# Reordering the opening of a two-layer diffusion backbone: order of loads, sums of squares, root, casts and low parts

## The reference

```
mod = split(silu(c) @ ada_w[0] + ada_b[0], 6)          # mod[0] shift, mod[1] scale
y   = x * rsqrt(mean(x * x, -1) + 1e-6) * norm1_g[0]
h   = y * (1 + mod[1]) + mod[0]
z   = gelu(h @ w_in)                                   # 1024 x 4096: halves u and v
v   = rmsnorm(z_v) ...;  y = (z_u * mixed(v)) @ w_out
```

## Time and profile before

| | |
|---|---|
| median of 3 runs | 1839.9 us (1839.88 to 1840.04) |
| the profiled execution's own time | 1837.93 us |
| its span, first to last instruction | 1836.1 us |
| mean granted TensorE clock | 0.999 |
| busy share PE, DVE, ACT, POOL | 99%, 83%, 53%, 25% |
| DMA, mean over the span | 205 GB/s |

### The profile page before, as it was taken

How to read it: one execution, slowest core, us unless ns; L and a number is a source line. 1 busy time by engine, 2 the same in 40 slices (tenths; PEclk the granted TensorE clock), 3 DMA queues, 4 the chain that set the end, 5 groups by cost and what they waited for, 6 DMA issues and landing times.

```text
span 1836.1 us, 35178 instructions
## 1 busy us (share of the span) xinstructions
PE 1822.6 (99%) x11716; PEld 1584.0 (86%) x11716; DVE 1520.1 (83%) x2819; ACT 966.7 (53%) x1631; POOL 454.0 (25%) x229
## 2 busy tenths in 40 slices
PE   8999999999999999999999999999999999999998
PEld 7999988888888888888889998888888888888887
DVE  6775889989998888888888589998999888885555
ACT  6754455665555444445555545565555544445554
POOL 6046588950000000000000368893000000000000
PEclk9999999999999999999999999999999999999999
DMA  9866455556554555588874455556655555555553
GB/s 383 330 237 220 161 187 191 184 199 218 203 179 163 182 172 176 186 308 320 323 254 161 161 170 184 191 185 207 218 194 171 171 173 174 180 172 194 193 190 132
DMA packets 104327, 376.40 MB, mean 205 GB/s; under 512 B 12481, under 2 KB 12737, under 8 KB 104001
## 3 DMA queue, kind: packets, MB, share of 16 engines
q1 hardware_dynamic: 103248, 373.11, 59.1%
q0 software_dynamic: 432, 2.10, 0.3%
q10 hardware_dynamic: 576, 0.32, 0.1%
HBM read 374.43 MB, written 1.05 MB: 204 GB/s over the span
## 4 chain that ended last, share of the span: by engine, by line
PE 91%; DVE 4%; DMA 2%; ACT 1%; POOL 1%; issue 0%; SPq 0%; ACTq 0%; DVEq 0%; POOLq 0%
PE ring L1882 22%; PE O L1935 13%; PE O L1937 13%; PE O L1936 13%; PE ring L1880 6%; PE ring L1887 6%; PE ring L1844 3%; PE ring L1587 2%; PE ring L1588 2%; PE ring L1589 2%; DMA raw<-in_u 2%; PE ring L1870 2%; PE ring L1849 1%; PE O L1870 1%; DVE wL L959 1%; ACT wH L574 1%
## 5 line engine op out<-in xcount | busy, mean ns | idle before, releaser
L574 ACT ACTIVATE wH<-raw 128x1024 fp32r<-128x1024 f32 x597 | 633.3, 1061 | 789.6 <-DMA raw<-in_v 361.6
L959 DVE TENSOR_TENSOR wL<-raw,wH 128x1024 fp32r<-128x1024 f32 x384 | 470.1, 1224 | 171.0 <-ACT wH L574 166.2
L1882 PE MATMUL ring<-hX,wH 128*128 128x512 f32 x1984 | 482.6, 393 | 0.0
L1882 PEld LDWEIGHTS ring<-hX,wH 128*128 128x128 f32 x1984 | 362.0, 188 | 69.5 <-issue 0.7
L1935 PE MATMUL O<-wH,gateH 128*128 128x512 f32 x1024 | 402.3, 393 | 0.2
L1937 PE MATMUL O<-wH,gateL 128*128 128x512 f32 x1024 | 398.9, 390 | 0.0
L1936 PE MATMUL O<-wL,gateH 128*128 128x512 f32 x1024 | 398.5, 389 | 0.0
L526 POOL TENSOR_TENSOR wL<-raw,wH 128x1024 fp32r<-128x1024 f32 x128 | 321.3, 2519 | 46.7 <-ACT wH L574 45.7
L1937 PEld LDWEIGHTS O<-wH,gateL 128*128 128x128 f32 x1024 | 192.2, 188 | 40.7
L1936 PEld LDWEIGHTS O<-wL,gateH 128*128 128x128 f32 x1024 | 192.4, 188 | 39.2
L1935 PEld LDWEIGHTS O<-wH,gateH 128*128 128x128 f32 x1024 | 192.3, 188 | 39.2 <-DVE gateL L1459 0.6
(11 more groups left out here) (227 smaller groups left out, 2469.4 us busy)
## 6 DMA issues: line engine op xcount, KB each, us to landing
raw<-in_u SPq DMA_DIRECT2D x256, 512.0 KB, 3.2
raw<-in_v SPq DMA_DIRECT2D x256, 512.0 KB, 3.3
ada_v<-in_ada SPq DMA_DIRECT2D x40, 512.0 KB, 4.4
raw<-in_w_q SPq DMA_DIRECT2D x30, 512.0 KB, 3.2
ada_m<-in_ada SPq DMA_DIRECT2D x24, 512.0 KB, 5.2
raw<-in_w_in SPq DMA_DIRECT2D x23, 512.0 KB, 4.3
ada_f<-in_ada SPq DMA_DIRECT2D x16, 512.0 KB, 15.1
raw<-in_w_out SPq DMA_DIRECT2D x16, 512.0 KB, 3.6
```

Source lines behind the costliest of these rows:

```text
L574: nc.scalar.activation(wH[s % RAW][:, :], (place or raw[s % RAW])[:, :], ACT.Copy).then_inc(s_h, 1)
L959: nc.vector.tensor_tensor(wL[s % RAW][:, :], raw[s % RAW][:, :], wH[s % RAW][:, :].bitcast(fp32), ALU.subtract).then_inc(s_low, 1)
L1882: ins = mm(bank[:, :], wH[s][:, k * P:k * P + P], hX[:, k, :, :].rearrange("p two t -> p (two t)"), start=(not low_weights_first and k == ...
```

## The change

The tokens come in two transfers of four tiles each, with a semaphore each, and ScalarE waits for each half before its squares. VectorE adds squares in four instructions, (0,1), (2,3), (4,5) and then the first two sums, and PE averages four tiles (3, 5, 6, 7) in place of eight; the six fillers before the means are gone. ScalarE takes the root before the cast of g0. For k = 0 VectorE multiplies token, gain and inverse root in one instruction, and ScalarE's scaling is left out. VectorE takes the ada sums earlier against the low parts of h. GpSimd makes half tiles in the order (0,s,0), (1,s,0), (0,s,1), (1,s,1), (2,s,0), (2,s,1), and PE counts them in that order. ScalarE's casts of g12 to g15 wait for PE too. SP issues f0 before g0, g4, g7 and g10 two places earlier, g12 before m16 and m17, g13 before m18, g14 before m19, and the six small loads after g15.

```
-            sp.dma_start(XT[:, :, :], xt_d).then_inc(s_x, 16)
+            for x in range(2):
+                sp.dma_start(XT[:, 4 * x:4 * x + 4, :], xt_d[:, 4 * x:4 * x + 4, :]).then_inc(s_x[x], 16)
             for g in range(4):
+                load_front(4 * g)
                 if g == 0:
                     load_gate(0)
-                load_front(4 * g)
                 load_front(4 * g + 1)
-                load_gate(3 * g + (g == 0))
+                if g:
+                    load_gate(3 * g)
+                load_gate(3 * g + 1)
                 load_front(4 * g + 2)
                 load_front(4 * g + 3)
-                if g:
-                    load_gate(3 * g + 1)
                 load_gate(3 * g + 2)
-            for dst, src in small_loads:
-                sp.dma_start(dst, src).then_inc(s_small, 16)
             m = ADA_FRONT
             for t in range(BLOCK_TILES, 16):
+                load_gate(t)
                 if t == BLOCK_TILES:
                     load_early(m)
                     m += 1
                 if t < BLOCK_TILES + 3:
                     load_early(m)
                     m += 1
-                load_gate(t)
+            for dst, src in small_loads:
+                sp.dma_start(dst, src).then_inc(s_small, 16)
...
-                    for t in range(BLOCK_TILES):
-                        front_low(t)
+                    for s in range(4):
+                        for half in range(2):
+                            front_low(3 * s, half)
+                            front_low(3 * s + 1, half)
+                        for half in range(2):
+                            front_low(3 * s + 2, half)
...
-            act.wait_ge(s_x, 16)
             for j in range(KT):
+                if j % 4 == 0:
+                    act.wait_ge(s_x[j // 4], 16)
                 square(j)
+            root(0)
             split_high(W_V, 0, 0)
-            root(0)
...
-                act.wait_ge(s_rooted, k + 1)
-                act.wait_ge(s_gain, 2 * k + 1)
-                nc.scalar.activation(sq[:, k, :], sq[:, k, :], ACT.Copy, scale=gs[:, 0, k:k + 1]).then_inc(s_xn, 1)
+                if k:
+                    act.wait_ge(s_rooted, k)
+                    act.wait_ge(s_gain, 2 * k + 1)
+                    nc.scalar.activation(sq[:, k, :], sq[:, k, :], ACT.Copy, scale=gs[:, 0, k:k + 1]).then_inc(s_xn, 1)
...
+            for n, (a, b) in enumerate(((0, 1), (2, 3), (4, 5), (1, 3))):
+                dve.wait_ge(s_sq, b + 1)
+                if n == 3:
+                    dve.wait_ge(s_pairs_sq, 2)
+                nc.vector.tensor_tensor(sq[:, b, :], sq[:, a, :], sq[:, b, :], ALU.add).then_inc(s_pairs_sq, 1)
             dve.wait_ge(s_row, 2)
...
             ada_front(0)
+            inverse_root(0)
             ada_front(1)
-            inverse_root(0)
-            dve.wait_ge(s_x, 16)
+            for x in range(2):
+                dve.wait_ge(s_x[x], 16)
             dve.wait_ge(s_rstd, 1)
-            rooted(0)
+            dve.wait_ge(s_gain, 1)
+            nc.vector.scalar_tensor_tensor(sq[:, 0, :], XT[:, 0, :], gs[:, 0, 0:1], O[1][:, 0:T], ALU.mult,
+                                           ALU.mult).then_inc(s_xn, 1)
             rooted(1)
+            low_h(0, 0)
             ada_front(2)
-            low_h(0, 0)
             ada_front(3)
-            for k in (2, 3, 4):
+            for k in (2, 3):
                 rooted(k)
             low_h(0, 1)
+            for k in (4, 5, 6, 7):
+                rooted(k)
             ada_front(4)
-            for k in (5, 6, 7):
-                rooted(k)
             ada_front(5)
-            for k in range(3, KT):
-                low_h(0, k - 1)
+            ada_front(6)
+            low_h(0, 2)
+            ada_front(7)
+            low_h(0, 3)
+            for k in range(4, KT):
                 ada_front(2 * k)
                 ada_front(2 * k + 1)
-            low_h(0, KT - 1)
+                low_h(0, k)
...
-                    pe.wait_ge(s_first_l, 2 * n + kk + 1)
+                    pe.wait_ge(s_first_l, 6 * s + (4 + kk if g == 2 else 2 * kk + g) + 1)
...
-            keep_clock(6)
-            for j in range(KT):
-                mean(0, j)
+            for j in (3, 5, 6, 7):
+                pe.wait_ge(s_sq, j + 1)
+                if j < 6:
+                    pe.wait_ge(s_pairs_sq, {5: 3, 3: 4}[j])
...
```

More of the change, by code:

```diff
@@ L196, in build @@
         s_bias = sem("s_bias")
-        s_x = sem("s_x")
+        s_x = [sem(f"s_x{x}") for x in range(2)]
         s_keys = sem("s_keys")
@@ L236, in build @@
         s_rooted = sem("s_rooted")
+        s_pairs_sq = sem("s_pairs_sq")
         s_xn = sem("s_xn")
@@ L513, in low_out, with front_low @@
                 nc.gpsimd.tensor_tensor(wL[s][:, :], raw[s][:, :], wH[s][:, :].bitcast(fp32), ALU.subtract).then_inc(s_l1, n)
-            def front_low(t):
+            def front_low(t, half):
                 pool.wait_ge(s_h, t + 1)
[L518 to L521, removed]
+                at = half * HALF
+                src = front_raw[t - 3] if t in FRONT_RAW else raw[t % RAW]
+                nc.gpsimd.tensor_tensor(wL[t % RAW][:, at:at + HALF], src[:, at:at + HALF],
+                                        wH[t % RAW][:, at:at + HALF].bitcast(fp32), ALU.subtract).then_inc(s_first_l, 1)
             def low_whole(base, i, s):
@@ L638, in front_high @@
             def front_high(t):
+                if t >= RAW:
+                    act.wait_ge(s_pe, t - RAW + 1)
                 if t in FRONT_RAW:
                     act.wait_ge(s_fraw[t - 3], 16)
-                    if t >= RAW:
-                        act.wait_ge(s_pe, t - RAW + 1)
                     nc.scalar.activation(wH[t % RAW][:, :], front_raw[t - 3][:, :], ACT.Copy).then_inc(s_h, 1)
@@ L1734, in _ @@
                     ins.then_inc(s_row, 1)
-            keep_clock(6)
-            for j in range(KT):
-                mean(0, j)
+            for j in (3, 5, 6, 7):
+                pe.wait_ge(s_sq, j + 1)
+                if j < 6:
+                    pe.wait_ge(s_pairs_sq, {5: 3, 3: 4}[j])
+                for tt in range(TT):
+                    ins = mm(O[tt][:, 0:P], sq[:, j, tt * P:tt * P + P], mean_w[:, :], start=(j == 3), stop=(j == KT - 1))
+                    if j == KT - 1:
+                        ins.then_inc(s_ms, 1)
             keep_clock(6)
@@ L1751, in _ @@
                         if s == 0:
-                            pe.wait_ge(s_rooted, KT)
+                            pe.wait_ge(s_rooted, KT - 1)
                         gate_block(2, s, 0)
```

## The result

| | before | after |
|---|---|---|
| median of 6 runs each, same chip | 1840.57 us (1839.88 to 1841.56) | 1848.21 us (1846.11 to 1853.59) |
| the profiled execution | 1837.93, span 1836.1 | 1850.07, span 1848.3 |
| mean granted clock | 0.999 | 0.997 |

The ratio is 1.0041, with a 95% interval of 1.0031 to 1.0052: slower by 7.6 us, where the forecast was 1844.0 with a range up to 1846.4. The sign and the place (the wait for u0) were right; the loss is almost twice as large.

What follows compares the result with a forecast made beforehand. Bound: u0, late behind a full queue. Late u0 and slips +2.4, clock fall +1.7, together +4.1 on the profiled 1837.93: 1842.0; the median lies 2.0 above that execution, so 1844.0 us, range 1840.6 to 1846.4.

Steps and rivals of the forecast that it cites:

- The sign and the place: Slower, chance 0.50; PE waits for u0 and starts the up projection at 65.7, 2.1 us later than before.
- The bound: Before the up projection: u0 comes late behind a full queue, so a sooner front gains 0.44 us at most.
- The means at the lower level: PE's opening: 16 passes at 0.234 us, 3.7 in all, means done at 11.8.
- ScalarE's start on the activation of k = 2: On the way to block (0,1,1): ScalarE starts at 23.6, activation at 24.4, cast of tile 4 at 25.4.
- Block (0,1,1): Middle of the front: starts at 28.1 instead of 28.98, between 26.2 and 29.0, waiting for a low half of tile 3.
- the second fall: Before the up projection: PE idles 2.9 us and the clock falls, costing 1.7, between 0 and 3.0.
- the rival of two falls: The clock falls also at the stop before block (0,1,1), delaying g12 and u0 by 1.5: +5.6, 1845.5 us, chance 0.08.
- Opening: Start of the kernel: the first half of the tokens lands 1.28 us earlier, at 5.0; the squares end at 7.6.
- The first block: PE's first gate block, after the means: at 15.8 instead of 16.78, with ends of 13.6 and 17.
- The first fall: A clock fall at PE's stop before block (0,1,1), delaying g12 and u0 by 1.5; a rival, chance 0.08.
- the restart: Queue dry from 43.4, g12 issued at 43.6 and landing 3.2 later; engines start again at 45.5, 2.1 us lost.
- the term of 0.4: Queue behind g15: the large small loads, six issues later, add some 0.4 us to u0's landing at 63.3.

Runs made afterwards that it cites:

- e2: Changed kernel with the tokens in one transfer again, all else as changed; median 1849.17 us, ratio 1.0045 to the kernel before.
- e6: Kernel before with only the tokens split into two transfers; ratio 1.0003 to the kernel before.
- e7: Changed kernel with the tokens in one transfer and SP's late loads in the order of before; ratio 1.0016 to the kernel before.
- e4: Changed kernel with 14 filler matmuls on PE ahead of the up projection, where it waits for u0; median 1846.68 us, ratio 1.0032.
- e9: e7 with 14 matmuls of one column added in the pause before the means; 1844.2 us, ratio 1.0016 to the kernel before.
- e11: e7 with the means as before: six fillers, eight tiles averaged, no additions on VectorE; ratio 1.0001 to the kernel before.
- e1: Changed kernel with SP's late loads back in the order of before; median 1845.27 us, ratio 1.0021 to the kernel before.
- e3: Kernel before with only SP's late loads in the new order; median 1846.42 us, ratio 1.0040 to the kernel before.
- e13: Kernel before with 20 front fillers replaced by 6 wider ones of the same total columns, TensorE's program 14 instructions shorter; ratio 1.0010.

## Why the prediction was too small, by its own steps

**What held.** The bound (u0 behind a full queue), the mechanism (g12's wait holds loads that need none; the queue runs dry; u0 late; PE stops; the clock falls), the low half for which block (0,1,1) waits, and ScalarE's start on the activation of k = 2 (23.6 forecast, 23.60). The means at the lower level (3.7 forecast, 3.76) held too, in part by luck: the same opening ran them at the full level in e2.

**Which steps failed.** Three in front of the up projection, and one that was missing. The changed kernel's profile gives the sizes of the three. Block (0,1,1) came 1.2 later than forecast, and a fall of the clock that had a chance of 0.08 cost 1.6 there; 0.3 was made up, so that g12 was issued at 46.12 in place of 43.6. From there u0 took 1.2 longer than the sum had. Together the up projection starts at 69.48 in place of 65.7, 5.9 later than before; with 1.5 for the second fall that is the 7.4 of 74 us, where the forecast was 4.1. What came is the rival of two falls, priced at 5.6, with 1.2 more for the block and 1.2 more for the queue, less 0.6 that was made up or came out smaller.

**Opening: a landing that was assumed.** The first half of the tokens was put 1.28 earlier, at 5.0. It landed at 6.15, when the whole had landed before (6.29); by itself this cost no time (e6). The first block, 16.25 for 15.8, lies inside the ends given; that the same opening can end between 14.9 and 17.5 is what e2 and e7 add.

**Block (0,1,1): a term mis-sized.** From 23.6 I took 0.8 to the end of the activation of k = 2. Gain, scaling, shift and activation stand in a row on ScalarE: 1.98 by the rows above, 23.60 to 25.58. Everything behind slipped: 29.26 for 28.1, and the 0.9 that g12 was to gain was gone.

**The first fall: given 0.08.** A stop of 1.9 before that block was followed by a fall in five of the seven profiles that have it (the changed kernel, e2, e4, e9, e11; not e1 and e7), a stop of 1.3 to 1.5 in none of six. Of stops inside the kernel the rows of before had shown only that 1.43 is survived, and those at its end that a fall can follow 1.23. "Only 0.7 longer than a stop that was survived" was therefore no argument for a chance under one half. What sets the two apart from the five stays open.

**The queue: the restart and the term of 0.4.** From the issue of g12 to the cast of u0 the prediction had 19.7 us (63.3 less 43.6). The four profiles with the late order took 20.4 to 22.5: the changed kernel 20.9, e3 the most. The landings of e3 show where it goes. From g11 to g12 there are 3.75 between landings, 2.5 more than a tile's 1.28, where the sum for the dry queue was 2.1. Behind that I let the transfers run at their old pace, with 0.4 for the little loads. From g12 to u0 e3 took 18.75 us for 12 tiles, 15.4 at 1.28 each (the changed kernel 17.1). Of the 3.4 lost, 1.8 stand at `bs` and `ws`, directly behind the four little loads (before, behind a full queue, the three tiles around the same loads lost 0.3); 0.6 at a tile during which an instruction packet of 16 KB ran. The rest is spread over tiles that SP issued one by one, each after its wait.

**The second fall: right.** It was in the forecast at 1.7; by the matmuls it cost 1.5. e4 takes it away, and its profile is 2.1 nearer to before at 75 us (5.3 behind in place of 7.4), 0.6 of which is an earlier u0.

**What was in no step.** The change takes 14 instructions out of TensorE's program ahead of loops that come 400 us later. I counted what the means cost in time and not that the program moves. By e13 that is 1.2 us [0.2, 3.5].

**The sum again.** By the medians: late loads 5.9 (e3), the program's length 1.2 (e13), the token split 0.3 or nothing (e6): 7.4 of 7.6. That this comes out so well is luck. By the ratios the same three are 7.4, 1.8 and 0.6, more than the whole, and each has an interval 3 to 5 us wide. Nor do the parts add up elsewhere: taking the late order out of the changed kernel (e1) gains 2.9 and not 5.9, and e7, with the additions, the level of the means, the half-tile order and the shorter program, is 3.5 above before and not the 1.2 of e13. So what these other parts cost is not settled.

## What to carry to other kernels

A load that must wait belongs behind every load that need not, on a queue that runs in order; and once such a queue has run dry, count not only the latency of the restart (2.5 here) but a slower pace after it (1.8 and 3.4 over 12 tiles here). Before a chain through several engines is priced, write down each instruction of it on the engine that is late: four short ones were priced as little more than one here. Where a gain ends in a wait for a transfer that is late already, as at u0, look first at what the edit does to that transfer.

## What the hardware showed that was not expected

- The program's own code moves over the same DMA engines as the data. A 16 KB packet of the instruction queue mostly took 0.9 to 1.3 us, and in the front of before the tile landing beside one (18.25) came 2.62 behind the tile ahead of it in place of 1.28. Behind 80 us every issue of a load that took SP more than 0.7 us, 41 in sixteen profiles, overlapped such a packet. Where the packets fall moved with 14 instructions in the front, and a wait 400 us later with them (e9, e13).
- Each fall of the clock in the middle of these runs lasted 3.41 us. It cost 1.5 to 1.6 where PE worked all through it, in e3 1.3, where PE stood still for its first 0.6.
- A matmul of one column cost 0.213 us a pass at the lower level (5.97 for 28 passes in e9), as much as the fillers of 128 columns there (2.52 for 12 in e1).
- The first half of a transfer cut in two landed at 6.15 to 6.33 (four profiles), the whole at 6.19 to 6.95 (twelve); the second half came 1.2 to 1.3 behind the first.
